# Output projection spread over the page stages of a hybrid decoder step, with row transposes between projection groups

## The reference

```python
z = einsum('btd,de->bte', rmsnorm(x, ln1), w_in)       # u, q, k, v, q_idx, k_idx, w_idx
pool_out = pool_mix(hist, u, ...)                      # windows 2, 4, 8, 16
attn_out = attend(q, gathered k, gathered v)           # prompt: own keys; sample: cache pages and own keys
h = x + einsum('bte,ed->btd', concat([pool_out, attn_out]), w_out)
a = square(relu(einsum('btd,df->btf', rmsnorm(h, ln2), w_ff1)))
y = rmsnorm(h + einsum('btf,fd->btd', a, w_ff2), ln_f)
```

## Time and profile before

| | |
|---|---|
| median of 3 runs | 1509.12 us (1508.16 to 1512.04) |
| the profiled execution | 1509.88 us, span 1508.1 us |
| TensorE matmuls busy | 1374.5 us (91%) |
| weight loads | 1274.3 us (84%) |
| VectorE busy | 684.7 us (45%) |
| ScalarE busy | 455.8 us (30%) |
| GpSimd busy | 493.6 us (33%) |
| chain that ended last | PE 69%, DVE 9%, ACT 5%, issue 3%, SPq 3% |
| mean granted TensorE clock | 0.978 |

### The profile page before, as it was taken

One profiled execution on the slowest core, in us unless ns is written; L12 is line 12 of the kernel. 1 busy time (PEld: TensorE's weight loads), 2 busy tenths in 40 slices (PEclk: granted clock), 3 DMA queues, 4 the chain that ended last, 5 costly groups with the idle time before them and its releaser, 6 DMA issues.

```text
span 1508.1 us, 24825 instructions
## 1 busy us (share of the span) xinstructions
PE 1374.5 (91%) x9469; PEld 1274.3 (84%) x9469; DVE 684.7 (45%) x1441; ACT 455.8 (30%) x985; POOL 493.6 (33%) x349
## 2 busy tenths in 40 slices
PE   1879969799878877999999999999999999999996
PEld 1856969798555666888899999999999999999996
DVE  4318997788977523011743323233232332323244
ACT  4324775664655522222522011020110201102043
POOL 3130773232442100222233433343333433343600
PEclk9989989999999999999999999999999999999999
DMA  5150111330001078775111111111111111111102
GB/s 170 38 127 0 43 50 29 100 86 15 1 1 29 16 231 249 235 247 176 42 44 43 43 51 48 43 43 43 56 42 43 43 50 49 42 43 49 64 15 102
DMA packets 129737, 107.06 MB, mean 71 GB/s; under 512 B 19848, under 2 KB 108808, under 8 KB 129615
## 3 DMA queue, kind: packets, MB, share of 16 engines
q1 hardware_dynamic: 118686, 98.49, 21.8%
q10 hardware_dynamic: 10281, 5.15, 1.2%
q0 software_dynamic: 656, 1.84, 0.5%
HBM read 94.57 MB, written 9.20 MB: 69 GB/s over the span
## 4 chain that ended last, share of the span: by engine, by line
PE 69%; DVE 9%; ACT 5%; issue 3%; SPq 3%; DMA 1%; POOL 0%; DVEq 0%; ACTq 0%
PE bank L1786 66%; ACT sjunk L988 3%; DVE junk L1441 2%; PE bank L1923 2%; SPq L497 2%; SPq L498 1%; DVE prob L1532 1%; DVE lack L1445 1%; DVE hn_lo L1654 1%; DVE cand L1451 1%; DMA page<-in_cache_k_dram 1%; PE bank L2066 1%; DVE cum L1500 1%; DVE probT L1566 1%; ACT probT L907 0%
## 5 line engine op out<-in xcount | busy, mean ns | idle before, releaser
L802 POOL TENSOR_TENSOR w_hi<-w_raw,zero 128x1024 fp32r<-128x1024 f32 x60 | 113.5, 1892 | 443.3 <-PE bank L1786 420.3
L1786 PE MATMUL bank<-hn_hi,w_hi 128*128 128x384 f32 (+1 forms) x768 | 249.5, 325 | 3.3 <-issue 1.8
L1786 PE MATMUL bank<-hn_lo,w_hi 128*128 128x384 f32 (+1 forms) x768 | 248.1, 323 | 0.0
L1786 PE MATMUL bank<-hn_hi,w_lo 128*128 128x384 f32 (+1 forms) x768 | 247.2, 322 | 0.0
L1786 PE MATMUL bank<-hid_hi,w_hi 128*128 128x384 f32 (+1 forms) x672 | 217.7, 324 | 0.0
L1786 PE MATMUL bank<-hid_lo,w_hi 128*128 128x384 f32 (+1 forms) x672 | 217.2, 323 | 0.0
L1786 PE MATMUL bank<-hid_hi,w_lo 128*128 128x384 f32 (+1 forms) x672 | 216.3, 322 | 0.0
L1221 ACT ACTIVATE relu<-relu 128x384 f32<-128x384 f32 (+1 forms) x96 | 47.8, 499 | 554.2 <-DVE relu L1720 554.2
L1735 DVE TENSOR_TENSOR acc<-bank,acc 128x384 f32<-128x384 f32 x168 | 87.0, 523 | 207.4 <-PE bank L1786 207.4
L1786 PE MATMUL bank<-xn_hi,w_hi 128*128 128x384 f32 (+1 forms) x456 | 151.0, 331 | 1.3 <-DVE score L1382 1.3
L804 POOL TENSOR_TENSOR w_lo<-w_raw,w_hi 128x1024 fp32r<-128x1024 f32 x60 | 150.0, 2499 | 4.7
(11 more groups left out here) (258 smaller groups left out, 2397.4 us busy)
## 6 DMA issues: line engine op xcount, KB each, us to landing
w_raw<-in_w_ff_dram SPq DMA_DIRECT2D x64, 512.0 KB, 3.8
page<-in_cache_k_dram SPq DMA_DIRECT2D x64, 256.0 KB, 3.0
page<-in_cache_v_dram SPq DMA_DIRECT2D x64, 256.0 KB, 3.3
w_raw<-in_w_in_dram SPq DMA_DIRECT2D x18, 512.0 KB, 3.6
xrow<-in_x_prompt_dram SPq DMA_DIRECT2D x8, 512.0 KB, 8.0
w_raw<-in_w_out_dram SPq DMA_DIRECT2D x8, 512.0 KB, 5.1
xblk<-in_x_prompt_dram SPq DMA_DIRECT2D x8, 512.0 KB, 4.3
out_dram<-yrow SPq DMA_DIRECT2D x8, 512.0 KB, 2.6
```

Source lines behind the costliest of these rows:

```text
L802: nc.gpsimd.tensor_tensor(w_hi[n[0] % 2][:, :], w_raw[n[0] % 2][:, :], zero_w, ALU.add).then_inc(s_whi, 1)
L1786: return nc.tensor.matmul(out, lhsT, rhs, start=start, stop=stop)
```

## The change

- **Rows.** to_rows is called for one piece at a time, after each token group of the next block; ScalarE copies a piece right after that group, ahead of the count.
- **Weight split.** For the 27 blocks of the input and output projection, GpSimd splits a block in four quarters of 256 columns, high and low in turn. The MLP's blocks are split as before.
- **Output projection.** Blocks 0 to 3 (k_tiles) are computed in the key stage, one tile after each unit but every fourth; blocks 4 to 7 (v_tiles) in the value stage, where value units follow tiles by the table v_upto, so that all 16 are used by the tenth of twelve tiles. The tiles in the key stage use banks 6 and 7, the page transposes three banks (3 to 5) instead of four.
- **Loads.** x blocks lie where the keys were and are loaded without the sample rows, which come once as a whole (xs_row). x and weight blocks stand between pages from the second unit on, by the tables x_at and w_at. The first two MLP weight blocks are issued before the last units are done.
- **Sample part and MLP start.** Squares of blocks 0 to 3 are added beside those of 4 to 7. The sample tokens' products stand after the first and second MLP tile, and the MLP's first tiles run in the order (0,0), (0,1), (1,0), (1,1), (0,2), (1,2), block and token group.
- **Last stage.** y_out stands ahead of a tile instead of behind it on ScalarE and VectorE.

The diff, cut to its core:

```diff
+        KM = C4
+        k_tiles = [(m, g) if g < 3 else None for m in range(KM) for g in range(4)]
+        v_tiles = [(m, g) for m in range(KM, KC) for g in range(3)]
+        v_upto = [min(G * NPG, (8 * t + 12) // 5) for t in range(len(v_tiles))]
-                    take(("kT", g, p, j), 3 + j)
+                    take(("kT", g, p, j), 3 + (BG * p + j) % 3)
+        for t in range(3 * KM):
+            take(("proj", N_OUT + t // 3, t % 3), 6 + t % 2)
...
+        first_tiles = [(0, 0), (0, 1), (1, 0), (1, 1), (0, 2), (1, 2)] + [(i, g) for i in range(2, FG) for g in range(3)]
...
+            x_at = {1: 0, 3: 1, 6: 2, 10: 3, 12: 4, 16: 5, 20: 6, 24: 7}
+            w_at = {2: 2, 4: 3, 8: 4, 12: 5, 16: 6, 20: 7}
+            for i in range(2 * G * NPG):
+                if i == 1:
+                    sp.wait_ge(s_pvu, NU)
+                if i in x_at:
+                    x_load(x_at[i])
+                if i in w_at:
+                    w_load(sp, N_OUT + w_at[i])
...
+                unit_load(i)
...
-                nc.gpsimd.tensor_tensor(w_hi[n % 2][:, :], w_raw[n % 2][:, :], zero_w, ALU.add).then_inc(s_whi, 1)
+                for i in range(WQ):
+                    c = slice(i * WP, i * WP + WP)
+                    nc.gpsimd.tensor_tensor(w_hi[n % 2][:, c], w_raw[n % 2][:, c], zero_w[:, 0:WP], ALU.add).then_inc(s_whi, 1)
...
             for i in range(FG):
                 if i == 1:
-                    pool.wait_ge(s_nl, 3 * KC)
+                    pool.wait_ge(s_nl, 2 * KC)
...
+                    if rows_dst is not None:
+                        rows_out(n - 1, rows_dst, g)
                     if g < 2 or n % 4 == 0:
                         count()
...
+                    if rows_src is not None:
+                        to_rows(n - 1, rows_src, g)
...
+            for i in range(G * NPG):
+                if i + 1 < G * NPG:
+                    page_T(i + 1)
+                sqk(i)
+                if k_tiles[i]:
+                    if i == 0:
+                        pe.wait_ge(s_olo, 2 * QB)
+                    out_tile(*k_tiles[i], 0)
+                    out_tile(*k_tiles[i], 1)
...
+            for t, (m, g) in enumerate(v_tiles[:-2]):
+                out_tile(m, g, 0)
+                out_tile(m, g, 1)
...
+                for i in range(v_upto[t - 1] if t else 0, v_upto[t]):
                     s_pv_(i)
...
+            for i, g in first_tiles:
                 pe.wait_ge(s_wlo, N_FF + i + 1)
...
+                if (i, g) == (0, 0):
+                    sample_out()
+                if (i, g) == (0, 1):
+                    sample_out_T()
+                    h_sums(0)
...
             for q, (g, i, m) in enumerate(last_tiles):
                 b, e, (t0, w) = q % LT, 2 * i + m, TG[g]
+                if g and e >= 5:
+                    y_out(3 * (g - 1) + e - 5)
```

More of the change, by code:

```diff
@@ L571, in down_load @@
                 sp.dma_start(dst, wf2[s, i]).then_inc(s_w[n % 2], 16)
-            for i in range(FG):
+            for i in range(2, FG):
                 up_load(0, i, N_FF, 0)
@@ L1708, in _, with ff_low @@
                 wait_evac(dve, ("R", g))
-            def ff_low(slot, q0, base_, r):
-                tiles = [(i, g) for i in range(FG) for g in range(3)]
+            def ff_low(slot, q0, base_, r, tiles=[(i, g) for i in range(FG) for g in range(3)]):
                 for q in range(len(tiles) + 1):
@@ L1836, in _ @@
             for n in range(3):
-                proj(n, xn_hi, xn_lo, 1)
-            to_rows(N_KI, qiT[:, 2, :])
+                proj(n, xn_hi, xn_lo)
+            for i in range(3):
+                to_rows(N_KI, qiT[:, 2, :], i)
             def kidx_T(b):
@@ L2108, in _ @@
[L2108 to L2118 removed]
+            out_tile(KC - 1, 1, 0)
@@ new lines, in _, with sample_out @@
+            out_tile(KC - 1, 1, 1)
+            so_T(1)
+            out_tile(KC - 1, 2, 0)
+            out_tile(KC - 1, 2, 1)
+            def sample_out():
+                wait_evac(pe, ("soT", G - 1))
+                pe.wait_ge(s_watt, 16)
+                for i in range(2):
+                    ps = begin(pe, ("smp", i))
+                    for c in range(C4):
+                        last = mm(ps[NS * c:NS * c + NS, :], sampT[:, c, :], w_att[:, c, 512 * i:512 * i + 512], True, True)
+                    last.then_inc(fullof(("smp", i)), 1)
@@ new lines, in sample_out_T @@
+            def sample_out_T():
+                pe.wait_ge(s_xs, 16)
+                for i in range(2):
+                    wait_evac(pe, ("smp", i))
+                ps = begin(pe, "smpT")
+                for k in range(KC):
+                    nc.tensor.matmul(ps[:, NS * k:NS * k + NS], xs_row[:, P * k:P * k + P], ident[0:NS, 0:NS],
+                                     start=k == 0, stop=False, is_transpose=True)
+                for k in range(KC):
+                    last = mm(ps[:, NS * k:NS * k + NS], smp_sb[:, P * k:P * k + P], hsum[:, :], False, k == KC - 1)
+                last.then_inc(fullof("smpT"), 1)
```

396 lines of the change are left out of this document (183 added, 213 removed).

## The result

The changed kernel takes 1466.53 us (median of 4 runs, 1463.4 to 1468.52), the kernel before 1509.51 us in the same comparison: a ratio of 0.9713, 95% interval 0.9700 to 0.9726, 43.0 us less. The forecast was 1470, range 1456 to 1485. The profiled execution took 1463.4 us (span 1461.6) and was the fastest of the four, so its stages add up to 46.5 us less than those of before, 3.5 more than the medians.

The account below looks back on a forecast made before the run. TensorE, busy 91% of 1508.1 us, was taken to bound the kernel, so only its waits and low clock counted. Terms of -24.8, -17.2, +8.2, +4 and -9.5 sum to -39.3 us: forecast 1470 us, range 1456 to 1485.

Parts of the forecast that it names:

- The forecast case: Whole kernel: all predicted terms together, -39.3 us, giving 1470 us; chance 0.63.
- rows between groups: Input projection: TensorE's waits for ScalarE's row copies and the low clock after them go, 1 us new wait; -24.8 us.
- key stage: Key page loading: output tiles moved in let pages come before they are wanted, only the first wait stays; -17.2 us.
- value stage: Value page loading: SyncE issues the last units too late, new TensorE waits of 6.5 us and a low-clock restart; +8.2 us.
- start of the MLP: First MLP tiles: VectorE's 1/rms chain begins after the sample part, so TensorE waits for the first bank; +4 us.
- last stage: End of kernel: output rows scaled before the tile free banks one tile earlier, removing 8.4 us of waits; -9.5 us.
- The residual wait: Input projection, near 204 us: TensorE still waits for ScalarE's copy of the third group; 1 us, bounds 0 and 4.
- 128x7 steps below 0.8 us except beside pooling sums: Expected sign: VectorE's small search steps are short with the quartered split, except beside GpSimd's pooling sums.
- (a): Value pages are fed in time and the 1/rms chain hides behind the sample work: 1458 us; chance 0.19.
- (b): Input projection: row waits return as waits for ScalarE, giving 10 of 24.8 us: 1485 us; chance 0.12.
- (c): The keys' stage stays bound by DMA; at 150 GB/s 29 us more: 1499 us; chance 0.03.
- (d): SyncE stands before weight blocks until GpSimd has split earlier ones, pages queued behind: slower, 1518 us; chance 0.03.

Follow-up runs that it names:

- the square of runs: The changed kernel against three versions of it: weight split at full width (1471.18 us), row transposes and copies back behind the groups (1486.84), both undone (1491.62).
- x_behind: Changed kernel with x block 0 issued one unit later, behind the pages of key unit 1 instead of ahead of them: 1464.15 us, ratio 0.9712.
- numbers_early2: Changed kernel with 16 page numbers (value units 4 to 7) read into registers in a row before SyncE stands for those slots: 1462.11 us, ratio 0.9680.

## Why the prediction was right

The forecast case came: row waits gone, page waits of the key stage gone but the first, new waits in the value stage and at the start of the MLP. By its own terms, in us of the profiled executions:

| term | predicted | measured |
|---|---|---|
| rows between groups | -24.8 | 222.2 to 196.3: -25.9 |
| key stage | -17.2 | -19.7 |
| value stage | +8.2 | +6.1 |
| start of the MLP | +4 | +4.7 |
| last stage | -9.5 | 73.8 to 63.1: -10.7 |
| before the projection, attention | 0 | -0.9 |
| sum | -39.3 | -46.4 |

The three in the middle are from the windows, with the prediction's price for twelve tiles and an estimate of about 4.6 us for the sample part, which moved into the MLP: key stage 77.0 + 51.2 (twelve tiles) + 3.0 + 1.3 = 132.5 before, 112.8 after; the rest of the output projection 126.9 - 51.2 - 1.3 - 4.6 = 69.8 before, and 77.0 - 1.1 (the first probability transposes, which lay ahead of that window before) = 75.9 after; MLP 711.8 - 702.5 - 4.6. The medians moved by 43.0, mostly because the profiled execution of the changed kernel was 3.1 us faster than its median.

**Rows.** Right, and the square of runs shows it causally: 25.1 us by medians. The residual wait, the step that was least sure, was put at 1 us with bounds 0 and 4; it is 1.87, at 203.7 us, for the vchunk copy of the third group, at the place that the prediction named. With the wide split it was 6.2 (4.4 for vchunk and 1.8 for vrow). The trace's chain has at that place three counts of ScalarE behind VectorE's slow steps, as foreseen. The sign "128x7 steps below 0.8 us except beside pooling sums" holds step by step: 6 of the 62 steps are longer, 1.67 to 2.45 us, and each lies beside a pooling sum of 1.9 or 2.5 us on GpSimd. Before, 25 of 62 were longer, most of them beside a full-width w_hi or w_lo.

**Key stage.** Mechanism right, size 2.5 us short. The waits fell by 10.9 (17.2 to 5.8, with 0.5 for ScalarE's copy of pageT as a new one), close to the 12.2 less 1 for the x block. The term that was mis-sized is the low clock. The prediction counted the restart after the 2.29 us wait (1.7 us), the only one after the ten later waits, and left the one after the first wait as it was. But that one shrank. The stretch behind the first wait, before and after, as windows:

```profile
530.78:537.00 6.22, 6.22 (x51) 5.25 (x52) 1.38 (x2) 1.19 (x2) 0.00 (x0) 0.52 0.79 235
...
505.35:510.00 4.65, 4.65 (x50) 4.18 (x50) 1.38 (x2) 1.19 (x2) 0.00 (x0) 0.70 0.99 324
```

By the granted clock it cost an estimated 6.22 x 0.48 = 3.0 us before and 4.65 x 0.30 = 1.4 after; why it is shorter stays open. And the x blocks without the sample rows were priced at nothing. The third tile of a block took 3.60 us (0.39 us of x transposes and the 3.21 of the earlier trace rows); in the chain of the changed kernel (start, us, what) it takes 3.47, since twelve of its matmuls are 256 columns wide instead of 288:

```profile
525.88 0.37 PE bank L2091 x2
526.25 3.09 PE bank L1813 x25
529.35 1.78 PE bank L2012 x16
```

Over eight blocks that is about 1 us, half of it in this stage. Some 0.7 us of the stage stay unexplained.

**Value stage.** Mechanism right, 2 us too dear. The step that was off is SyncE's pace: it went on at 1.13 us a page, 4.5 a unit, from a stretch where SyncE also waited for slots (0.6 us) and in single issues (up to 1.27 us instead of 0.33). Undisturbed, a page takes 1.09 us from start to start, in that stretch as in this one, so twelve units take about 52.3 us instead of 54. The first register load is in the 8.5 us after which the fifth unit's first page was issued (618.16 - 609.68), where the prediction had 7.7 + 0.7. Three blocks stood between the pages, 2.4 us in all, where two for 1.5 us were counted. So the last page was issued at 671.8 and was in at about 674.9 (3.1 us to landing, as in the earlier trace rows), 65.3 us into the stage where the prediction had 67.0; TensorE wanted it 61 us into the stage without its waits, not 59.8. The Trainium skill (DMA: Bandwidth & Descriptors, Latency and other measured facts) has the 600 ns floor from which the prediction estimated 0.93 us a page; the measured 1.09 is nearer to the 1.13 that I took, and the pages came late, as forecast. TensorE's waits are 3.7 us instead of 6.5 (2 to 10), and the low clock cost about 2.2 instead of 1.7. Constant page numbers remove 5.9 us, which shows the cause.

**Start of the MLP.** Right: first bank free at 719.84, 33.2 us after the first MLP tile (33 said), TensorE there 29.8 us after it (29 said); 3.35 us of wait, where 4 was said, and 1.6 of low clock, which had no term (48 matmuls from 719.84 took 10.2 us where 8.6 is usual). Two small waits of before, 0.94 and 0.48 us, went and had no term. That makes 3.5 us, 1.2 less than the table's 4.7; part of this may be the 4.6, which is an estimate, and no run settles the rest.

**Last stage.** Right; the stage gave 10.7 in one execution and 8.9 by medians of the kernel with it undone, around the 9.5.

**Rivals.** (a) did not come: value pages made TensorE wait in every trace with the numbers read one by one (3.7 to 6.3 us in eight kernels), and the MLP wait was 3.3 or 3.4 us, 2.1 in x_behind, wherever the chain was left as it was. (b) did not come: the projection has no wait for ScalarE but the 1.87. (c) did not come: 230 GB/s were moved beside the tiles, far over 150. (d) did not come: SyncE does stop before four of the six weight blocks between the pages, about 5 us each time, but not one of these stops reached TensorE in the key stage, where only the first unit was waited for.

## What to carry to other kernels

A wait can be covered or its cause removed, and the two are worth different things: here moving tiles under the page loads, with what moved along, brought 9 us, while the cause, about half a microsecond of SyncE for the page number in front of each DMA, was worth 18 in the old kernel, and without it the new order cost 4, all of it at the start of the MLP. Take the price of an issuing queue from start to start of its issues, in a stretch in which it doesn't wait: the length of a row of issues leaves out what lies ahead of the first. When one engine's queue carries both a search and the copies that free banks, put the copies ahead of the search steps; this was worth four times as much as making the search steps faster.

## What the hardware showed that was not expected

The DMA share of a window is no linear scale: 0.83 went with 245 GB/s, 0.98 with 355 and 1.04 with 398. VectorE's 128x7 instructions took 48.4 us in sum beside full-width GpSimd instructions and 27.5 beside quarter-width ones, although GpSimd was busy longer with the quarters (116.5 against 101.0 us). And not every stop costs clock: with the 2.1 us wait for a value page in numbers_early2 the value stage's granted clock is 1.00, while the 2.54 us wait of the changed kernel was followed by a tile of 5.75 us where 4.46 is usual.
